# mLSTM steps of a hybrid decoder: the second dense run of each step moved ahead of the state update, which then stands beside the next transposes

## The reference

```python
def step(carry, inp):
    C, n, m = carry
    ...
    w_intra = jnp.exp(dmat - m_t[..., None])
    w_inter = jnp.exp(inter - m_t)
    a = jnp.einsum('blhd,bshd->bhls', qc, kc) * w_intra
    num = (jnp.einsum('bhls,bshe->blhe', a, vc)
           + jnp.einsum('blhd,bhde->blhe', qc, C) * w_inter.transpose(0, 2, 1)[..., None])
    den = jnp.sum(a, axis=-1) + w_inter * jnp.einsum('blhd,bhd->bhl', qc, n)
    ...
    C_new = decay[..., None, None] * C + jnp.einsum('bhs,bshd,bshe->bhde', wk, kc, vc)
    ...
proj = (xn @ w_in).astype(F32)
...
out = (jax.nn.sigmoid(o) * h.reshape(B, S, H * DV)).astype(xn.dtype) @ w_out
```

## Time and profile before

| | |
|---|---|
| median of three runs | 2380.61 us (2378.47 to 2381.62) |
| profiled execution, its time | 2380.01 us |
| its span | 2378.2 us |
| PE busy | 2320.1 us, 98% of the span |
| DVE busy | 1476.4 us, 62% |
| ACT busy | 977.4 us, 41% |
| POOL busy | 318.1 us, 13% |

### The profile page before, as it was taken

The page is one execution under the profiler, slowest core; times in us unless marked ns, Lnnn a source line. Parts: engine busy times, 40 slices in busy tenths (PEclk is TensorE's granted clock), DMA queues, the critical chain, the costliest instruction groups (busy, mean ns, idle before and its releaser), DMA issues.

```text
span 2378.2 us, 41213 instructions
## 1 busy us (share of the span) xinstructions
PE 2320.1 (98%) x16214; PEld 2219.5 (93%) x16214; DVE 1476.4 (62%) x2597; ACT 977.4 (41%) x1978; POOL 318.1 (13%) x333
## 2 busy tenths in 40 slices
PE   7999999999999999999999999999999999999998
PEld 7899898878999999999999877869999999999998
DVE  6555555569856566566566676465856656566564
ACT  4233222235534344343343354254634335334345
POOL 2000000013111111111112011013011111111113
PEclk8999999999999999999999999999999999999999
DMA  3112121101121121111112312101111111121121
GB/s 119 45 45 61 49 68 31 47 27 46 36 63 45 39 67 35 53 53 35 53 53 61 98 32 52 35 11 37 44 54 54 36 53 53 35 62 44 43 63 74
DMA packets 160984, 119.72 MB, mean 50 GB/s; under 512 B 23623, under 2 KB 140276, under 8 KB 160836
## 3 DMA queue, kind: packets, MB, share of 16 engines
q1 hardware_dynamic: 160724, 118.10, 17.0%
q10 hardware_dynamic: 144, 0.02, 0.0%
HBM read 110.94 MB, written 12.33 MB: 52 GB/s over the span
## 4 chain that ended last, share of the span: by engine, by line
PE 71%; issue 20%; DVE 5%; POOL 1%; ACT 1%; DMA 0%; SPq 0%; POOLq 0%; DVEq 0%; ACTq 0%
PE acc L2623 9%; PE acc L2621 9%; PE acc L2622 9%; PE acc L2582 8%; PE acc L2581 8%; PE acc L2583 8%; PE acc L2690 3%; PE acc L2692 2%; PE acc L2691 2%; PE acc L2711 2%; PE acc L2559 1%; PE acc L2560 1%; PE acc L2561 1%; PE acc L2734 1%; PE acc L2722 1%
## 5 line engine op out<-in xcount | busy, mean ns | idle before, releaser
L2623 PE MATMUL acc<-h_hi,w_lo 128*128 128x352 f32 x1344 | 434.7, 323 | 0.0
L2621 PE MATMUL acc<-h_hi,w_hi 128*128 128x352 f32 x1344 | 434.0, 323 | 0.0
L2622 PE MATMUL acc<-h_lo,w_hi 128*128 128x352 f32 x1344 | 431.6, 321 | 0.0
L1528 DVE TENSOR_TENSOR x_res<-x_res,acc 128x1056 f32<-128x1056 f32 x224 | 280.5, 1252 | 126.1 <-PE acc L2623 125.8
L2622 PEld LDWEIGHTS acc<-h_lo,w_hi 128*128 128x128 f32 x1344 | 254.8, 190 | 0.0
L2582 PE MATMUL acc<-x_lo,w_hi 128*128 128x264 f32 x896 | 254.6, 284 | 0.0
L2583 PE MATMUL acc<-x_hi,w_lo 128*128 128x264 f32 x896 | 254.6, 284 | 0.0
L2581 PE MATMUL acc<-x_hi,w_hi 128*128 128x264 f32 x896 | 254.5, 284 | 0.0
L2621 PEld LDWEIGHTS acc<-h_hi,w_hi 128*128 128x128 f32 x1344 | 251.8, 187 | 0.0
L2623 PEld LDWEIGHTS acc<-h_hi,w_lo 128*128 128x128 f32 x1344 | 251.8, 187 | 0.0
L2338 PE MATMUL acc<-x_hi,w_hi 128*128 128x352 f32 x576 | 195.8, 340 | 2.5 <-DVE pair L1796 1.4
(11 more groups left out here) (351 smaller groups left out, 5364.7 us busy)
## 6 DMA issues: line engine op xcount, KB each, us to landing
w_raw<-in_w_up SPq DMA_DIRECT2D x64, 512.0 KB
w_raw<-in_w_down SPq DMA_DIRECT2D x64, 512.0 KB
w_raw<-in_w_mlstm_in SPq DMA_DIRECT2D x24, 512.0 KB
x_in<-in_x_prompt SPq DMA_DIRECT2D x8, 512.0 KB, 4.5
w_raw<-in_w_mlstm_out SPq DMA_DIRECT2D x8, 512.0 KB
w_raw<-in_w_q SPq DMA_DIRECT2D x16, 256.0 KB
w_raw<-in_w_attn_out SPq DMA_DIRECT2D x16, 256.0 KB
out_y_prompt<-y_out SPq DMA_DIRECT2D x8, 512.0 KB, 2.6
```

The costliest lines, as they stand in the source:

```text
L1528: V.tensor_tensor(blocks(x_res[:, k]), blocks(x_res[:, k]), row_banks(layer, k), ALU.add).then_inc(row_taken, 1)
L2621: T.matmul(out[:, b], hi[:, c], mh[:, span(b)], start=(c == 0), stop=False)
L2622: T.matmul(out[:, b], hi[:, c], ml[:, span(b)], start=False, stop=False)
L2623: x = T.matmul(out[:, b], lo[:, c], mh[:, span(b)], start=False, stop=(c == 1))
```

## The change

In every step the run B is issued right behind A, ahead of `part4(c - 1)` and `part3(c)`, which with `part1(c + 2)` now make one group. On VectorE its share of B comes ahead of `heads_out` and `update`. Nothing is added or removed; ACT, POOL and the transfers keep their orders.

```diff
@@ vector engine, units(pr)
                     numerators(c)
                     dense(window(pr, 3 * c + 3))
+                    dense(window(pr, 3 * c + 4))
                     if c > 0:
                         heads_out(c - 1)
                     if c == NCH:
                         dve.wait_ge(ht_taken, t0 + NCH)
                         gate(2)
                     update(c)
-                    dense(window(pr, 3 * c + 4))
                     normalise(c)
```

## The result

| | before | after |
|---|---|---|
| median | 2380.72 us (2378.47 to 2381.62, 4 runs) | 2397.2 us (2395.22 to 2398.35, 4 runs) |
| after / before | | 1.0069, 95% interval 1.0057 to 1.0082 |
| profiled execution, its time | 2380.01 us | 2398.35 us |
| its span | 2378.2 us | 2396.5 us |
| mean granted clock of the span | 0.994 | 0.988 |

What follows compares the result with a forecast made beforehand. TensorE, busy for 98% of the span, was taken as the bound. Gains and losses from waits and clock summed to +13.2 us on the profiled 2380.0, 2393.2; the median's 0.6 more gave 2394, range 2386 to 2399.

Steps and rivals of the forecast that it cites:

- grouping of the small matmuls: Steps 0 to 6 with B not empty: one group saves 0.04 us in each of 26 steps, -1.0 us.
- step 3 of pairs 1 and 2: VectorE takes its share of B earlier, so a dense matmul no longer waits: -0.3 us each, -0.6.
- steps 2 and 5 of pair 3: Where A ends a slab and B starts the next, B's second block finds the bank taken: 0.4 us each, +0.8.
- step 7, pairs 1 and 2, the wait: Dense matmul of C waits for VectorE's late block-taking, as `part3` comes two rows later: +2.9 us per pair, +5.8.
- clock behind the long waits: After stands of about 3.7 us in step 7, a stretch at 1.2 GHz costs 1.5 us each, +3.0.
- step 8, pair 0: The next pair's `part1` waits for `pair_start`, with C only two rows as cover: +1.3 us.
- `part4(8)` of pair 3: At pair 3's end it moves with the later state product and B's first row finds A's blocks untaken: +1.7 us.
- more drops: Rival: stands in step 8 or before pair 3 bring one or two more clock drops, 1.5 us each: 2396 to 2397; chance 0.15.
- The cover holds: Rival: VectorE's lists in steps 6 to 8 don't come late, only gains of 1.9 us remain: 2378.7; chance 0.07.
- Half of it: Rival: a step 7 term is shorter, 2.9 becomes 1.5, and no clock price: about +7 us, 2387; chance 0.1.
- A much dearer return: Rival: each group saved is worth far more than 0.04 us, 26 x 0.5 = 13 needed to draw level; chance 0.03.
- The clock price fails to come: Rival: step 7 idles of 3.7 us end without a drop or fall on cheap matmuls: 2391; chance 0.14.

Runs made afterwards that it cites:

- the early steps alone: Against before, the new order in steps 0 to 5 only, on both engines, steps 6 to 8 in the old order: 2377.37 us, ratio 0.9994.
- step 7 alone: Against before, the new order in step 7 of each pair only: 2389.39 us, ratio 1.0047.
- a list 2.6 us shorter: Against after, VectorE's step 7 list has `sample_inputs` and C's share straight behind `update`, then `normalise`, `gate`, `y_low`: 2385.46 us, ratio to before 1.002.
- after with `pair_start` earlier: Against after, `pair_start` stands ahead of `normalise` in VectorE's list of step 8: 2394.14 us, ratio to before 1.0055.
- early steps together with a reordered list: Against before: new order in steps 0 to 5 except pair 3's 2 and 5, step 7's list turned, pair 3's `exponents(8)` earlier in step 6: 2368.89 us.

## Why the prediction was right, point by point

The forecast was 2394, the result 2397.2. By the terms of the sum:

| term | predicted | measured |
|---|---|---|
| grouping of the small matmuls | -1.0 | mostly -0.01 to -0.10 a step, about -0.9 |
| step 3 of pairs 1 and 2 | -0.6 | -1.0 |
| step 4 of pair 3 | -0.3 | -0.4 |
| steps 2 and 5 of pair 3 | +0.8 | +1.1 |
| step 6 | +0.9 | +0.9 |
| step 7, pairs 1 and 2, the wait | +5.8 | +5.8 |
| step 7, pair 0 | +0.8 | +0.85 |
| clock behind the long waits | +3.0 | +5.1 |
| step 8, pair 0 | +1.3 | +1.4, and 1.6 of clock |
| pair 2 to 3 | +0.8 | +0.7 |
| `part4(8)` of pair 3 | +1.7 | +1.6 |

The terms of waiting were right to a few tenths, all of them. That their sum is right to 0.2 is in part luck: 0.4 more gained in step 3 and 0.3 more lost in steps 2 and 5 of pair 3 cancel. The rule of the prediction was that VectorE's work behind `part3` is late by B, less what leaves its list, less its slack. Three experiments bear it out: the early steps alone lose nothing, step 7 alone brings most of the loss, and a list 2.6 us shorter takes 2.6 us from the wait.

**The step that was mis-sized is the price of the clock.** The prediction took 1.5 us a drop from one place with 32 small matmuls; the bound it set, 1.7, was too low as well. In after each of the two drops of step 7 cost 5.44 - 2.88 = 2.6 us. The windows show what was off, the length of the stretch at 1.2 GHz and not the cost of a microsecond in it. Here are the place in before that the price was taken from, one of the two in after, and step 7 of pair 2 in after with `pair_start` earlier, where the drop cost 4.50 - 2.9 = 1.6:

```profile
528.20:531.60 3.40, 3.40 (x31) 2.67 (x28) 0.85 (x2) 0.00 (x0) 0.00 (x0) 0.50 0.00 0
...
316.90:323.70 6.80, 5.74 (x39) 4.47 (x39) 1.84 (x5) 0.00 (x0) 0.00 (x0) 0.50 0.01 2
...
447.00:450.40 3.40, 3.40 (x31) 2.55 (x31) 0.00 (x0) 0.00 (x0) 0.00 (x0) 0.50 0.02 5
```

The clock is low for 3.4 us in the first and the third, and that cost 1.4 and 1.6; it is low for 6.8 us in the second, 1.06 of them still within the stand, and that cost 2.6. The prediction's row was read rightly, but it held one short stretch, and step 7 of after got long ones.

A third drop, behind a wait of 0.91 us ahead of pair 1, brought 1.6. That is the rival *more drops*, which came on top of the forecast, and the 3.6 us by which the table's measured sum, 16.8, lies above 13.2 are for the most part 2.1 for the first two and 1.6 for the third. The prediction had a row for it: before has a low clock behind the 1.77 us ahead of pair 3 (0.50 from 459.9 to 463.3 us), which it didn't look up when it called that stand only "of that size". The remaining difference up to the 18.3 us between the spans is the low clock in an MLP and small things behind the mLSTM. Which drops the other three executions of after have isn't known, as only one is profiled; their times, 2395.2 to 2398.3 us, go with mean clocks of 0.991 to 0.988, where the 46 executions of before that the experiments were compared with have 0.991 to 0.995.

**The grouping.** Right in sign and size. A group in after, pair 3, step 2:

```profile
498.29 0.38 PE L2437 MATMUL acc<-ident,h_n 128*128 128x128 f32 x2
498.60 0.44 PE L2420 MATMUL acc<-v_aug,k_w 128*64 128x129 f32 x4
498.97 0.33 PE L2359 MATMUL acc<-ident,pair 128*128 128x128 f32 x1
...
500.08 0.43 PE L2338 MATMUL acc<-x_hi,w_hi 128*128 128x352 f32 x1
```

498.29 to 500.08 is 1.79 us, where the earlier trace rows has 1.80, and L2359 starts 0.20 behind the last of the four matmuls of L2420, slightly over the 0.09 to 0.17 that the prediction named as a sign. The prediction weighed there what the Trainium skill's page "TensorE: Matmul & The Clock Gate", section "Step-by-step: what each phase is for", says of weight loads that are pulled ahead, and drew from it that this term would be nothing. The trace doesn't bear that reading out: the kernel with the early steps alone gives about -0.04 in nearly every step. What the 0.11 us of a return consists of no run shows.

**The rivals.** *The cover holds* falls with the waits of 3.56 us. *Half of it* falls too. *A much dearer return* falls with the 1.79. *The clock price fails to come* isn't what happened in after. It happened at one of the two places in step 7 alone and at one of the two in after with `pair_start` earlier, but at both places in none of the three traces. That the small gains exist and are worth about 2 us in all is shown by the first experiment.

**What stays open.** What decides whether a wait of 3.56 us is followed by a low clock, and for how long. Over after, step 7 alone and after with an earlier `pair_start` there are six such waits with the same kinds of dense rows ahead of them; in three the clock was low for 6.8 us, in one for 3.4, in two it stayed at 1.00. A drop ahead of pair 3 in before (0.59 from 460 to 464 us), behind an idle of 1.77 us, is absent in five of the experiments with the same idle; there the step is 1.6 us shorter.

## What to carry to other kernels

Before work that covers a wait is moved from behind a release to ahead of it, count the list of the engine that is released, from there to the first thing that the busy engine needs back, for each kind of step and not for the usual one: here 21 of the 24 early steps were covered or nearly so, and step 7 had 5 us of list against a cover of 2.2. If such a list is too long, its order is the cheaper lever: what the other engine waits for goes first, and what nobody waits for (`y_low`, the decay terms) goes last. Here the change as a whole lost 16.5 us, and its early steps together with a reordered list gained 12.

## What the runs showed of the chip that wasn't expected

The granted clock behind one and the same wait differs from place to place and from kernel to kernel: 3.56 us and 0.59, 3.57 us and 1.00 within one trace. The Trainium skill's page "TensorE: Matmul & The Clock Gate", section "What's actually happening", says that what the gate looks at runs on by itself and isn't set off by the kernel, so that the place of the change varies from run to run. The six waits are in accord with that; no run here shows what the gate looks at.

A drop has no one price, and the length of the stretch at 1.2 GHz goes with it. Stretches of 3.4 us cost 1.6 us: behind a wait of 0.91 us ahead of pair 1 of after (204.2 to 207.6 us), and behind one of 3.56 in the kernel with `pair_start` moved (447.0 to 450.4 us). Stretches of 6.8 us, which begin 1.0 to 1.5 us before the wait of 3.56 us ends, cost 2.5 to 2.6: two in after (316.9 to 323.7 and 450.0 to 456.8 us) and one in step 7 alone (312.4 to 319.2 us). A stand of 3.56 us thus cost its own length and 0, 1.6 or 2.6 us more.

Executions of one and the same kernel differ by as much. The 46 executions of before in the experiments take from 2377.0 to 2386.0 us, with a mean granted clock of 0.995 in the fastest and 0.991 in the slowest. So small terms are read from the steps, with the clock of each stretch beside them, and not from the spans.
